# First block's heads beside the panels of both projections, in a new column order, with a 1024 wide gate modulation and a row-order output projection

## What is computed

```python
# first block
mod = silu(c) @ ada_w + ada_b            # six rows of 2048: sh1, sc1, g1, sh2, sc2, g2
u = rms_norm(x, g) * (1 + sc1) + sh1
proj = u @ w_in                          # 5919 columns: q, k, v of four kinds of attention
o = concat(fox(7 heads), nsa(8 heads: selected + window + compressed keys, gated),
           dilated(9 heads, weighted by their lse), diff(4 heads, two maps each, sub-norm))
h = x + g1 * (o @ w_out)
h = h + g2 * swiglu(rms_norm(h, g') * (1 + sc2) + sh2)
x = rms_norm(h, final_norm_g)
# second block: two layers of pooling or attention, memory attention, gates, layer norm
```

## Time and profile before

| | us |
|---|---|
| median of 3 runs | 2204.05 (2201.49 to 2206.65) |
| the profiled execution | 2203.98 |
| its span, first to last instruction | 2202.3 |
| `win`, first to last low half | 214.5 to 347.9 |
| `win_end` | 349.0 to 429.6 |
| `wout` | 551.9 to 666.2 |
| TensorE, VectorE, ScalarE busy over the span | 2085.6, 1448.2, 1061.6 |

### The profile page before, as it was taken

The page is one execution under the profiler, slowest core; times in us unless marked ns, Lnnn a source line. Parts: engine busy times, 40 slices in busy tenths (PEclk is TensorE's granted clock), DMA queues, the critical chain, the costliest instruction groups (busy, mean ns, idle before and its releaser), DMA issues.

```text
span 2202.3 us, 28516 instructions
## 1 busy us (share of the span) xinstructions
PE 2085.6 (95%) x9820; PEld 1717.6 (78%) x9820; DVE 1448.2 (66%) x2502; ACT 1061.6 (48%) x1945; POOL 83.7 (4%) x182
## 2 busy tenths in 40 slices
PE   6997999997897999999999999999999899999996
PEld 5776888876676887888888888788788788888885
DVE  5987988656898877565555655854465655555556
ACT  3544444465334444445544454454354555555542
POOL 2000000221003000000000000000000000000000
PEclk9998999998898999999999999999999999999998
DMA  8999999434795897566656665574456455555562
GB/s 312 367 369 291 373 367 332 125 91 129 282 335 184 294 291 261 190 193 191 190 186 196 191 191 184 178 247 136 133 184 220 147 159 172 172 163 174 171 221 94
DMA packets 312952, 478.28 MB, mean 217 GB/s; under 512 B 32736, under 2 KB 136896, under 8 KB 311424
## 3 DMA queue, kind: packets, MB, share of 16 engines
q1 hardware_dynamic: 310064, 460.76, 64.2%
q0 software_dynamic: 2768, 15.98, 2.2%
HBM read 465.13 MB, written 2.10 MB: 212 GB/s over the span
## 4 chain that ended last, share of the span: by engine, by line
PE 80%; DVE 8%; issue 6%; SPq 3%; DMA 2%; ACT 2%; POOL 0%; DVEq 0%; POOLq 0%; ACTq 0%
PE ps L508 24%; PE ps L510 24%; PE ps L509 24%; SPq L868 3%; DVE w_lo L440 2%; DVE ada_acc L452 1%; PE ps L1559 1%; PE ps L998 1%; PE ps L976 1%; PE ps L757 1%; DMA raw<-in_w_out 1%; ACT w_hi L393 1%; PE ps L541 1%; PE ps L468 1%; DMA X<-in_x 0%
## 5 line engine op out<-in xcount | busy, mean ns | idle before, releaser
L440 DVE TENSOR_TENSOR w_lo<-raw,w_hi 128x512 fp32r<-128x512 f32 (+1 forms) x1328 | 902.1, 689 | 649.5 <-ACT w_hi L393 644.2
L393 ACT ACTIVATE w_hi<-raw 128x512 fp32r<-128x512 f32 (+1 forms) x1328 | 829.6, 629 | 1001.1 <-PE ps L510 947.7
L508 PE MATMUL ps<-w_hi,actT 128*128 128x512 f32 (+1 forms) x1920 | 767.8, 400 | 24.1 <-DVE w_lo L440 16.5
L510 PE MATMUL ps<-w_hi,actT 128*128 128x512 f32 (+1 forms) x1920 | 750.7, 391 | 0.0
L509 PE MATMUL ps<-w_lo,actT 128*128 128x512 f32 (+1 forms) x1920 | 750.2, 391 | 0.0
L508 PEld LDWEIGHTS ps<-w_hi,actT 128*128 128x128 f32 x1920 | 364.2, 190 | 105.7 <-DVE w_lo L440 14.8
L510 PEld LDWEIGHTS ps<-w_hi,actT 128*128 128x128 f32 x1920 | 363.5, 189 | 76.4
L509 PEld LDWEIGHTS ps<-w_lo,actT 128*128 128x128 f32 x1920 | 364.3, 190 | 73.2 <-issue 1.4
L508 PE MATMUL ps<-w_hi,hidT 128*128 128x512 f32 x352 | 138.4, 393 | 3.0 <-DVE w_lo L440 3.0
L510 PE MATMUL ps<-w_hi,hidT 128*128 128x512 f32 x352 | 137.2, 390 | 0.0
L509 PE MATMUL ps<-w_lo,hidT 128*128 128x512 f32 x352 | 137.2, 390 | 0.0
(11 more groups left out here) (265 smaller groups left out, 1562.1 us busy)
## 6 DMA issues: line engine op xcount, KB each, us to landing
raw<-in_w_in SPq DMA_DIRECT2D x216, 512.0 KB, 4.3
raw<-in_ada_w SPq DMA_DIRECT2D x192, 512.0 KB, 5.8
raw<-in_w_out SPq DMA_DIRECT2D x96, 512.0 KB, 4.3
raw<-in_ffn_w_gate SPq DMA_DIRECT2D x176, 256.0 KB, 2.9
raw<-in_ffn_w_up SPq DMA_DIRECT2D x176, 256.0 KB, 3.1
raw<-in_ffn_w_down SPq DMA_DIRECT2D x88, 512.0 KB, 4.0
raw<-in_w_kv_shared SPq DMA_DIRECT2D x48, 512.0 KB, 3.6
raw<-in_w_mem_kv SPq DMA_DIRECT2D x32, 512.0 KB, 6.8
```

The lines of the kernel that those rows point to most:

```text
L393: act.activation(w_hi[:, g, 0:w], raw[:, slot_of(st, it), b, 0:w], ACT.Copy).then_inc(hi_ready, 1)
L440: nc.vector.tensor_tensor(w_lo[:, g, 0:w], raw[:, slot, b, 0:w], w_hi[:, g, 0:w].bitcast(f32), ALU.subtract).then_inc(blocks_read, 1)
L508: nc.tensor.matmul(o, hi, w_hi[:, g, 0:w], start=(k == 0), stop=False)
L510: last = nc.tensor.matmul(o, lo, w_hi[:, g, 0:w], start=False, stop=(k == nk - 1))
```

## The change

**Column order.** `w_in` is taken in the order of `WIN_K` and `WIN`, so that `win_k` brings the columns of nsa (q, compressed, selected and window keys and values) and the forget gates first, then dilated, diff, and fox last. `win` has nine panels (one of 480 and one of 320 columns) and `win_end` is gone.

**Heads beside panels.** The class `Attn`, the loops, the staging copies and the merge are gone. A class `Duo` has steps like those of `Pair`; 25 of them (12 of nsa, 5 dilated, 4 diff, 4 fox; of dilated and fox one head is done twice) start every six parts, from part 13 of 208 (`win` has parts 0 to 143, `wout` 144 to 207). They read q, k and v in `proj` directly, have one table buffer (GpSimd builds the next after `at_max` of the one before), and tiles of their own for `probs` and `probsT`. ScalarE copies both heads' probabilities. Gates and the factor of the second diff map go into the pair's reciprocals. `k_twice` holds keys that two heads share, twice. PSUM banks 4 to 6 are the pairs', bank 7 is for all small sums and turns.

**Modulation.** The columns of `g1` become A items, 1024 wide: eight beside the last panel of `win`, 24 beside `wout`; four row sums (`row_sum`) come in parts 165 to 197.

**Output projection.** Its rows are taken in the order `O1_ORDER`, so that the first rows are those whose heads are done first; the panels 0 and 1 run side by side, then 2, with the last rows of 0 and 1 within it, then 3. The turns of `o1` stand at parts 131 to 174. `gated_out` and `add_out` use two buffers and write X for both halves at once. The compression's weights `w1` are loaded after `memkv` and not after `win_k`.

```diff
+def wout_order():
+    weights = [(j, ch) for ch in O1_ORDER[:7] for j in range(2)]
+    weights += [(2, ch) for ch in O1_ORDER[:6]] + [(0, O1_ORDER[7]), (1, O1_ORDER[7])]
+    weights += [(2, ch) for ch in O1_ORDER[6:]] + [(3, ch) for ch in O1_ORDER]
...
+        if n < 24:
+            order.append(("A", 0, 8 + n, 0) if n < 8 else ("A", 0, n - 8, 1))
...
-    Stage("win", 1, [("wA", 16)] * 6), Stage("win_end", 1, [("wA", 16)] * 2 + [("w", 16)]),
-    Stage("wout", 2, [("wa", 16)] * 2),
+    Stage("win", 1, [("wA", 16)] * 9),
+    Stage("wout", 1, [("w", 16)] * 4, wout_order(), an_given=0, banks=(0, 2, 5, 0), turned=O1_ORDER, n0=144),
...
+        DUO_AT = [13 + 6 * i for i in range(len(DUOS))]
+        O1_TURN = (131, 136, 139, 142, 156, 158, 161, 174)
+        ROW_SUM = (165, 169, 194, 197)
...
-            pool.wait_ge(ada_taken, 1 + ST["win_k"].end[3])
+            pool.wait_ge(parts_used, HILO + ST["memkv"].end[1])
...
+            def duo_steps(n):
+                for duo, c in zip(DUOS, DUO_AT):
+                    if n == c - 3:
+                        duo.turn(pe)
+                    elif n == c:
+                        duo.scores(pe)
+                    elif n == c + 10:
+                        duo.turn_probs(pe)
+                    elif n == c + 13:
+                        duo.outputs(pe)
...
+                    if n == c + 2:
+                        duo.early(act)
+                    elif n == c + 10:
+                        duo.exps(act)
+                    elif n == c + 15:
+                        duo.copy(act)
...
+                    if n == c + 4:
+                        duo.maxima(dve)
+                    elif n == c + 13:
+                        duo.stats(dve)
+                    elif n == c + 16:
+                        duo.normed(dve)
+                if n - 5 in O1_TURN:
+                    low_o1(O1_TURN.index(n - 5))
+                if n - 5 in ROW_SUM:
+                    take_row(ROW_SUM.index(n - 5))
...
+            def normed(self, dve):
+                dve.wait_ge(S("at_rs"), self.i + 1)
+                dve.wait_ge(S("at_pv"), self.i + 1)
...
+            def turn_o1(s):
...
+                    pe.wait_ge(turn_taken, TURNS["o1"] + s)
...
+                last.then_inc(turned, 1)
```

More of the change, by code:

```diff
@@ L73, with __init__ @@
 class Stage:
-    def __init__(self, name, bodies, panels, order=None):
+    def __init__(self, name, bodies, panels, order=None, an_given=None, banks=None, turned=tuple(range(8)), n0=0):
         self.name, self.bodies, self.panels = name, bodies, panels
+        self.banks, self.n0 = banks, n0
+        self.place = {ch: s for s, ch in enumerate(turned)}
         self.local, self.items, self.sum_after = [], [], {}
@@ L104, in __init__ @@
         self.a_end = {i.a: i.off + 2 for i in self.items if i.kind != "w"}
-        self.split_banks = order is not None
+        self.first, self.last = {}, {}
+        for i in self.items:
+            if i.kind == "w":
+                self.first.setdefault(i.j, i)
+                self.last[i.j] = i
 def k_major():
@@ new lines, in program @@
+        DUOS = []
+        for _h in range(0, NSA, 2):
+            for _kind in ("slc", "win"):
+                DUOS.append(Duo(len(DUOS), _kind, _h, 0, 0))
+        for _h in range(0, NSA, 2):
+            DUOS.append(Duo(len(DUOS), "cmp", _h, 0, 0))
+        for _h in (0, 2, 4, 6, 7):
+            DUOS.append(Duo(len(DUOS), "dil", _h, 3, 3))
+        for _h in range(DIFF):
+            DUOS.append(Duo(len(DUOS), "diff", _h, 5, 6))
+        for _h in (0, 2, 4, 5):
+            DUOS.append(Duo(len(DUOS), "fox", _h, 8, 9))
@@ L1453, in _ @@
+            stage_matmuls(pe, "win", actT, width=WIN_W, sum_at=99, carry=True, each=beside_mixer)
+            stage_matmuls(pe, "wout", actT, each=beside_mixer)
             lead = turning(pe, "u2", lambda k, t: xn2[:, t, k * P:(k + 1) * P], quarter_ready("u2"))
@@ L1706, in _ @@
+            take_win = stage_copy("win", lambda p, j, t: proj[:, t, WIN[j]:WIN[j] + WIN_W[j]], width=WIN_W,
+                                  lead={0: lambda: take_k(0), 2: lambda: take_k(1), 5: lambda: take_k(2)}, defer=True,
+                                  each=beside_mixer)
+            stage_split_hi(act, "wout", each=beside_mixer)
             for i in range(3):
@@ L1888, in far @@
                 chain(v.tensor_scalar(dist[:, kk, :], di, 1.0, MASKED, ALU.min, ALU.mult))
-                chain(v.tensor_tensor(dist[:, kk, :], dist[:, kk, :], dist[:, 0, :], ALU.add))
+                v.tensor_tensor(dist[:, kk, :], dist[:, kk, :], dist[:, 0, :], ALU.add).then_inc(S("far"), 1)
             def fox_start():
-                dve.wait_ge(acc_read, 2 + ST["win"].end[2])
-                dve.wait_ge(S("cmp_in"), 16 * 8)
+                dve.wait_ge(acc_read, 2 + ST["win_k"].start[2] + 1)
+                dve.wait_ge(S("cmp_in"), 16 * 6)
                 fb = fox_b[:, :].unsqueeze(1).broadcast_to([P, T, FOX])
@@ L1975, in dilated_lse @@
             def dilated_lse():
[L1976 to L1979 removed]
+                dve.wait_ge(S("dil_kept"), 5)
                 chain(v.tensor_tensor(d9(0)[:, :, 0, :], nm[0], nm[1], ALU.min))
```

905 lines of the change are left out of this document (481 added, 424 removed).

## The result

| | before | changed |
|---|---|---|
| median | 2202.77 us (2199.37 to 2206.65, 4 runs) | 2179.72 us (2179.10 to 2180.97, 4 runs) |
| ratio, 95% interval | | 0.9901 [0.9886, 0.9916] |
| span of the profiled execution | 2202.3 | 2178.1 |
| first `w_lo` of `win` | 214.5 | 217.4 |
| TensorE's end of `wout` | 670.2 | 647.4 |

Faster, as forecast, but by 1% and 23 us and not by 61. The time is outside the range (2125 to 2172). A second set of runs of both kernels (`e15_changed_again`) gave 2198.17 and 2181.80 us, 16 us apart (0.9924 [0.991, 0.9937]); the kernel before varies more than the changed one, 2195.6 to 2206.7 us over all its runs. Nearly all of the miss is one number: the row takes 430 us where 378.9 + 11 were forecast. `win` starts 2.9 us later here (forecast 6), the tail saves 2.1 (1.6), the stages that the diff leaves alone are 0.7 us longer in sum.

The account below looks back on a forecast made before the run. Before, SyncE's staging copies end last in 122 us of attention; in the new row TensorE binds: 378.9 us work, 11 waits, 6 weight loads, 395.9 against 455.7. With the tail 61.4 us saved: 2143 us, range 2125 to 2172.

Parts of the forecast that it names:

- the tail: After `wout`, the last row sum and its addition leave the path: 1.6 us saved.
- 77.5 + 28.0 = 105.5 us: TensorE's work in the row beside weights: 25 head pairs 77.5 us, smaller pieces (modulation, compression, forget sums, turns) 28.0 us.
- the pair's price: TensorE's cost of a head pair between weight parts, read from the second block: 3.1 us, bounds 2.8 and 3.33.
- The rival with the loop's price: Pairs keep the old attention loop's 3.75 us on TensorE: 16 us more, 2159 us; chance 0.08.
- I went through the numbers in the new schedules: Check of waits within the row: answers mostly one to three parts early, five places not; 11 us, 0 to 30.
- (b) to (e): Waits: `o1` turn at 158, 1.5 us; VectorE overload 149 to 162, 3; gated sums 189 to 193, 2; X reload, 2.
- (b): The turn of `o1` at part 158 needs the low half written at VectorE's part 161: 1.5 us wait.
- 367 us, 97% of TensorE's: VectorE's work summed over the whole row of 208 parts, against TensorE's 378.9 us; TensorE stays the bound by a little.
- VectorE sets the pace: Rival: in the row six parts with a pair take 12.2 us, not 11.3; 22 us more, 2165 us; chance 0.17.
- the w1 load: The compression's two 512 KB weight loads, moved into `win_k`, delay `win`: 6 us, bounds 2.7 and 10.
- the table buffer: Rival: pairs wait for GpSimd's single position table, which would need 13.9 us or more; 2205 us or more; chance 0.05.
- The clock: Sign that the forecast is right: TensorE's clock at 2.4 GHz throughout both projections, no longer falling to 1.2 GHz after waits.

Follow-up runs that it names:

- e15_changed_again: The changed kernel unaltered, run once more beside the kernel before: 2181.80 us against 2198.17 us, ratio 0.9924.
- no heads: The changed kernel without the 25 head pairs' work on TensorE, ScalarE and VectorE (X's slices only zeroed, semaphores kept): 2095.75 us, the row 342 us.
- both edits: The changed kernel with scores and maxima one part later, and turns of `o1`, `gated_out` and `add_out` spread wider: 2165.56 us.
- the maxima's move: The kernel with later scores and spread turns, its maxima put back from c + 5 to c + 4 (c: a pair's part in `DUO_AT`): 2164.53 us.
- e2: The changed kernel with the gate modulation's 1024-wide sums in the last `win` panel and `wout` cut to 8 columns: 2170.08 us.

## Why the prediction was wrong

**The place of the gain** was right: the 122 us without panel matmuls are gone, DMA doesn't bind `win`, and of `wout` only some 11 us, and the row is mostly TensorE's weights and pieces. The pieces alone held, read as the prediction reads them: 77.5 + 28.0 = 105.5 us forecast, 104 measured over the row without the waits between their instructions.

**The step that failed** is the last one of the pair's price, "the start of the next matmul less that of the piece", with "25 x 3.1 = 77.5 us (70 to 83)". It counts up to the first next matmul and takes TensorE as back in its beat there. A pair costs the row 3.8 us (no heads, TensorE's parts 44 to 104): 3.04 of pieces, 0.36 of four late second matmuls, 0.33 ahead of the scores; 0.1 has no place. 25 x 0.7 is 18 us of the 40. The late second matmul was to be seen before. This is TensorE's timeline of the kernel before, behind the last piece of the earlier trace rows (its first matmul starts at 2024.39):

```profile
2024.71 0.40 PE L509 MATMUL ps<-w_lo,actT 128*128 128x512 f32 x1
2024.94 0.39 PE L510 MATMUL ps<-w_hi,actT 128*128 128x512 f32 x1
2025.17 0.39 PE L508 MATMUL ps<-w_hi,actT 128*128 128x512 f32 x1
```

The next starts lie 0.32, 0.23 and 0.23 us apart; I had read on only to the first. The bounds of 2.8 and 3.33 were both formed without it. The rival with the loop's price, 3.75 us a pair, had the better number for another reason.

**The step "I went through the numbers in the new schedules"** passed over the copy. scores(i) and the copy of pair i - 2 share the banks; the copy stands at ScalarE's part c + 3 of the new pair, which in the changed kernel it reaches too late for TensorE. By the timeline 3.3 us are lost ahead of the scores from 36 to 96 (44 steps from the stream to a piece, 0.301 us in the mean where 0.226 is usual; all of it at the scores). The sooner copy gave 2.3 there, so 0.23 us a pair are the wait for the copy, and the 0.1 that stays at each of the scores is another cost, of a cause not shown.

**A term left out.** The sum starts TensorE with the row, but the row is measured from VectorE's first low half (217.4 us), and TensorE still multiplies parts of `win_k` until 220.5: 3.1 us.

**The waits (b) to (e)**, 8.5 us, were mis-sized. The segments from 128 on are 16 us over; some 5 of these are the pairs' price and some 5 the three stretches at 1.2 GHz (both estimates). The other 6 come on top of the 8.5, and TensorE's waits for VectorE are indeed 13 us there. The sum of VectorE over the whole row, "367 us, 97% of TensorE's", hid that its load is uneven: the last `win` panel has 320 columns for TensorE, and the same A items for VectorE. It was the bound there (28.8 of 33 us busy, TensorE 27.4), which is the rival "VectorE sets the pace", but in 80 parts and not in all: cutting its late sums moved nothing between 36 and 128. Three of the turns of `o1` waited 2 to 3 us each, at parts 139, 142 and 158, where (b) named the last with 1.5. Spread turns, later scores and cut sums together bring this part from 159.4 to 139.8 us, more than the excess; the places of the work and its load have about 10 and 9 us of it, with two and one of the stretches at 1.2 GHz that went with them.

**Right by their terms:** the w1 load (6 forecast; 4.8 and, doubled, 6.6 by the start of `win`), the tail, the table buffer (no effect even with twice the work), and some places of the waits (158 and the sub-norm's; not 139 and 142).

**The clock** was not at 2.4 GHz throughout, and the sum had nothing for it: 0.95 or 0.96 is granted in four of the windows above. It is at 1.2 GHz for 3.4 us at 239.5, 522.8, 563.7 and 618.4 us, which at half rate costs up to 6.8 us of the 40, an estimate (before, the windows of the loops and of `wout` had 0.88 and 0.92). Ahead of the last three TensorE had been busy for 6.24, 7.02 and 7.42 of 10 us, with waits for VectorE in between; ahead of the first, in the compression, for 9.35:

```profile
512.80:522.80 10.00, 6.24 (x47) 6.00 (x48) 8.93 (x25) 2.65 (x6) 4.38 (x5) 1.00 0.75 258
553.70:563.70 10.00, 7.02 (x43) 5.50 (x44) 9.96 (x23) 3.39 (x11) 4.87 (x5) 1.00 0.71 243
608.40:618.40 10.00, 7.42 (x32) 5.52 (x32) 9.63 (x14) 4.39 (x8) 0.00 (x0) 1.00 1.04 394
```

**Open:** for the 8 us over in the first 16 parts no edit was tried; with no heads they are there as well (36.9 us). 3.1 of them are the start of TensorE and some 1.7 the stretch at 239.5 us; the rest belongs to the compression's pieces, or to how many parts TensorE is behind at the mark. Why the second matmul behind a piece is late, no run tells. Joining pieces saves little beside the waits: with scores later the joined piece takes 2.24 us where its two parts take 2.12, and saves the 0.09 us behind one of them and the 0.09 ahead of the scores (timeline, 36 to 96).

In sum, of the 40 us: pairs 18, the clock up to 7, waits for VectorE 6, the start 3; the last 6 are not placed.

The best version seen is both edits (2165.6 us, 1.6% under before, with or without the maxima's move), 14 us under the changed kernel.

## What to carry to other kernels

Price an insertion by the whole beat around it, from a stream matmul well ahead to one well behind, not up to the next start: here 0.1 us behind each of 116 pieces was 11 us in sum. When an edit is read as a difference of two stretches, both must hold the same work of the engine that binds: marks on VectorE gave 3.94 us a pair, TensorE's own starts 3.8. Add up the load of the second engine by panels and not over a stage, above all where panels differ in width, since the narrow one has the same side work for less cover. And look at the granted clock of a stretch before a difference of 1 to 3 us in it is put down to an edit: two profiles of one kernel agreed within 0.2 us behind part 16, yet kernels with the same work in a segment differed by 1.6 us there, by one stretch of 3.4 us at 1.2 GHz.

## What was not expected of the hardware

- GpSimd's table operation takes 1081 ns in the mean, beside a VectorE that is busy for 344 of 430 us, against 511 before and 835 with no heads. The prediction said that no row shows such a slowing; it came, and nobody waited for it. That is the direction of what the Trainium skill says ("GPSIMD Engine Reference", Specifications) of the interfaces shared with VectorE; that they are the cause here, no run shows. VectorE's 1024 wide sums went from 1278 to 1334 ns in the mean of the page, to 1421 in the last `win` panel.
- A `SCALAR_TENSOR_TENSOR` of 128 x 8 lasted 372 ns in e2's row above: cutting its width by 128 took away only three quarters.
- Half the size didn't cost TensorE half: eight score instructions with 64 contraction rows take 0.86 us against 1.12 with the second block's 128, and twelve output instructions 64 wide 1.26 against 1.25 with 128.
